# A two-part transformer kernel on one core: four edits around a joint feed-forward stage

## The chip, the cores and the metric

The kernel runs on 1 core of a Trainium2 chip, as one program and one launch. The metric is device time in microseconds (us), the median over runs. PE is the matrix engine, DVE the vector engine, ACT the scalar engine, POOL and SP here only issue DMAs.

## The reference, cut to what matters

There are 256 tokens of 1024 features (`x`) and 256 context tokens (`ctx`), all in fp32. Two models run one after the other; only the first has a context.

```
s_lat, s_ctx = silu(c), silu(c_ctx)
for l in 0, 1:                                  # first model
    six vectors for x from s_lat @ w_ada[l], six for ctx from s_ctx @ w_ada[l]
    h  = rmsnorm(x) * gain * (1 + scale) + shift             # the same for ctx
    conv branch: glu, depthwise conv, layernorm, silu;  attention branch over x and ctx
    x  = x + g1 * ((sigmoid gates * branches) @ w_out)       # ctx too where l = 0
    x  = x + g2 * (silu(u_g) * u_a) @ w_down,  u = conv3(norm(x) @ w_up)   # ctx too where l = 0
x = rmsnorm(x)
for l in 0, 1:                                  # second model
    half a swiglu, stick-breaking attention (l = 0) or a gated recurrence (l = 1), half a swiglu,
    each modulated by vectors from silu(c_2) @ mod_w[l]
return rmsnorm(x)
```

The vectors are small in output and large in weights: `s @ w_ada` and `s @ mod_w` read 120 blocks of 1 MB, which the kernel calls modulation blocks.

## The kernel before

**Matrix work.** Activations lie features by tokens. A weight is read in slabs, each of two halves. For each half ACT rounds the raw fp32 weights to a high part (`split_hi`, L744), DVE subtracts it from the raw ones for a low part (`split_lo`, L1333), and PE makes three matmuls for each 128x128 chunk: high by high, high by low, low by high (`mm3`, L2206 to L2208). Raw weights, high parts and low parts have two buffers each (slab parity p). SP loads the next raw half once the low part of the one before in its buffer is made. Each engine runs through one list of stages (`plan`) in the same order, with its own code for every stage kind. There is no scheduler: the order in which the code is written is the order on the engine, and a wait holds all that stands behind it.

**Modulation blocks.** Blocks 0 to 21 are multiplied on PE. From block 22 on each half block is one DVE instruction (`mod_product`, L1370: a 128x1024 multiply with a sum) on `modraw`, which has one buffer for each half; blocks below 32 need a second one for the context (L1367). POOL loads the next block's half into the buffer once the product of this half is done. A stage's `mods` says how many blocks it takes: 1 is one half block with each slab, 2 both halves. A product that finds its half not landed holds DVE.

**The places.** (a) The gated stage of the context (kind `gate`): attention heads beside the gate slabs, then a layernorm of the conv branch, whose four Silu on ACT (L1053) free the last chunks of the first `merge` slab. (b) A norm needs the sum of squares over 8 feature tiles. ACT squares, DVE adds some of the tiles (`add_squares`, L1524), and PE sums over partitions with a matrix of ones (`norm_sum`, L2261, fp32, one matmul for each tile that is left). Two norms of `x` are made ahead, during other stages: one in the context's `merge` stage, one in the stages `q` and `v` that make keys and values of the context for layer 1 (`norm_ahead`). (c) The joint feed-forward of layer 0 runs `x` and `ctx` together (512 columns) in two parts: 12 features of 22 through `upa` and `down`, then the other 10. In `upa` each slab gives one feature: ACT scales (L1172, L1174), DVE adds four conv taps (L2032), ACT takes a Silu (L1159), DVE multiplies (L2004), ACT rounds (L1180, for the last L1190), DVE makes the low part (L2010). The last two steps of a feature follow the taps of the next one. `joint_opening` is the first two slabs of `down` on PE. (d) In the last body of the second `down` part (`ctx_first`), PE makes the context's halves of slabs 6 and 7 first, then `x` of 6, the norm's sum, and `x` of 7. The norm of the context follows (`do_norm`, i = 4): root, eight scaled tiles (L1504), high parts on ACT (L833), low parts on DVE (L1513), for the keys' slab (`slab_after_norm`, L2533 to L2542). DVE's update of the residual is `joint_product` (L1888). (e) Stage `q` with `w_sbk` and stage `v` with `w_sbv` make keys and values of the stick-breaking attention. In the latter DVE's masks and sums (L1694, L1684, L1699) stand between the low parts and the modulation products.

## Time and profile before

| | us |
|---|---|
| median of 3 runs (2250.38 to 2251.74) | 2250.89 |
| the profiled execution | 2255.51 |
| its span, first to last instruction | 2253.5 |
| PE busy in it | 2167.5 (96%) |
| DVE busy | 1808.6 (80%) |
| ACT busy | 1246.7 (55%) |

The share of PE's clock that is granted is 0.986 over the span: it stands at 1.0 (2.4 GHz) or at 0.5 (1.2 GHz). Matmul ends are modelled, so a busy PE says less than the starts of its instructions and its idle times. An idle time is printed in brackets behind the instruction that ends it, with what released it.

### The profile page before, as it was taken

Reading aid. Unit: us, or ns where it says so; the run is one execution under the profiler, and the core shown is the slowest. Engines: PE = TensorE matmul, PEld = TensorE weight load, DVE = VectorE, ACT = ScalarE, POOL = GpSimd, SP = SyncE. Lnnn points to the kernel's source line nnn. Section 1 sums busy time; section 2 is a strip of 40 time slices with the busy share of each in tenths; the row PEclk is TensorE's granted clock in tenths of the full one; section 3 lists DMA queues with packets and bytes.
Section 4 is the critical chain, followed back from the end, with each engine's and each line's share of the span. In section 5 each row is a group of like instructions: output and inputs, shape, how many; then the busy total and the mean of one; then the engine's idle time right before and its main releaser. Section 6 shows DMA issues by size and latency. Waiting matters only on the chain.

```text
span 2253.5 us, 42557 instructions
## 1 busy us (share of the span) xinstructions
PE 2167.5 (96%) x15168; PEld 1984.7 (88%) x15168; DVE 1808.6 (80%) x3102; ACT 1246.7 (55%) x1981; POOL 120.4 (5%) x232
## 2 busy tenths in 40 slices
PE   7998999999999989999999999999999999999998
PEld 5897988888788779889999889997989989999898
DVE  4886797777677768978998988877988888889865
ACT  4466457544223333576664664656664655686653
POOL 0100000000010100000000001000010001000000
PEclk8999999999999999999999999999999999999999
DMA  9845553434475555535788688773788788636754
GB/s 360 284 132 172 182 175 127 151 130 133 137 261 184 180 178 172 178 118 166 239 271 275 227 282 266 231 245 122 246 277 272 230 280 279 232 125 192 243 177 132
DMA packets 139741, 465.59 MB, mean 207 GB/s; under 512 B 16208, under 2 KB 20432, under 8 KB 138064
## 3 DMA queue, kind: packets, MB, share of 16 engines
q1 hardware_dynamic: 102560, 339.41, 44.8%
q0 software_dynamic: 32688, 120.08, 17.1%
q10 hardware_dynamic: 4352, 4.20, 0.6%
q8 instruction: 92, 1.51, 0.3%
q14 instruction: 49, 0.40, 0.0%
HBM read 462.57 MB, written 1.05 MB: 206 GB/s over the span
## 4 chain that ended last, share of the span: by engine, by line
PE 74%; DVE 12%; ACT 6%; issue 4%; DMA 3%; ACTq 0%; SPq 0%; DVEq 0%; POOL 0%; POOLq 0%
PE bank_pair L2206 16%; PE bank_pair L2208 16%; PE bank_pair L2207 16%; PE bank_pair L2345 12%; PE bank_pair L2350 6%; DVE w_lo L1333 3%; DMA modraw<-in_w_mod 2%; DVE arena L1648 2%; ACT w_hi L744 2%; PE bank_pair L2335 2%; DVE small L1762 1%; PE ps_o L2219 1%; ACT arena L1011 1%; DVE arena L1823 1%; PE ps_o L2853 1%
## 5 line engine op out<-in xcount | busy, mean ns | idle before, releaser
L1333 DVE TENSOR_TENSOR w_lo<-raw,w_hi 128x1024 fp32r<-128x1024 f32 (+2 forms) x672 | 735.5, 1118 | 124.8 <-ACT w_hi L744 120.3
L744 ACT ACTIVATE w_hi<-raw 128x1024 fp32r<-128x1024 f32 (+2 forms) x672 | 640.5, 969 | 334.2 <-PE bank_pair L2208 193.1
L2206 PE MATMUL bank_pair<-e_both,w_hi 128*128 128x256 f32 (+1 forms) x1632 | 470.9, 289 | 11.3 <-DVE w_lo L1333 7.7
L2206 PE MATMUL bank_pair<-h_joint,w_hi 128*128 128x256 f32 (+1 forms) x1488 | 464.5, 312 | 8.1 <-DVE w_lo L1333 3.4
L2207 PE MATMUL bank_pair<-e_both,w_hi 128*128 128x256 f32 (+1 forms) x1632 | 464.1, 284 | 0.0
L2208 PE MATMUL bank_pair<-e_both,w_lo 128*128 128x256 f32 (+1 forms) x1632 | 464.0, 284 | 0.0
L2207 PE MATMUL bank_pair<-h_joint,w_hi 128*128 128x256 f32 (+1 forms) x1488 | 456.7, 307 | 0.0
L2208 PE MATMUL bank_pair<-h_joint,w_lo 128*128 128x256 f32 (+1 forms) x1488 | 456.5, 307 | 0.0
L2206 PEld LDWEIGHTS bank_pair<-e_both,w_hi 128*128 128x128 f32 x1632 | 314.9, 193 | 22.0 <-DVE w_lo L1333 9.9
L2207 PEld LDWEIGHTS bank_pair<-e_both,w_hi 128*128 128x128 f32 x1632 | 315.2, 193 | 0.3
L2208 PEld LDWEIGHTS bank_pair<-e_both,w_lo 128*128 128x128 f32 x1632 | 315.0, 193 | 0.0
L2206 PEld LDWEIGHTS bank_pair<-h_joint,w_hi 128*128 128x128 f32 x1488 | 285.4, 192 | 33.2 <-issue 14.1
L2345 PE MATMUL bank_pair<-h_joint,w_hi 128*128 128x512 f32 x1216 | 304.6, 393 | 0.1
L2207 PEld LDWEIGHTS bank_pair<-h_joint,w_hi 128*128 128x128 f32 x1488 | 285.7, 192 | 12.9
L2208 PEld LDWEIGHTS bank_pair<-h_joint,w_lo 128*128 128x128 f32 x1488 | 285.5, 192 | 12.4
L1370 DVE SCALAR_TENSOR_TENSOR modraw<-modraw,cact 128x1024 f32<-128x1024 f32 x196 | 238.1, 1220 | 32.5 <-DMA modraw<-in_w_mod 32.2
L2345 PEld LDWEIGHTS bank_pair<-h_joint,w_hi 128*128 128x128 f32 x1216 | 218.8, 189 | 39.2 <-DVE e_plain L1473 0.3
L693 POOL DMA_DIRECT2D modraw<-in_w_mod x216 | 114.1, 529 | 1954.2 <-DVE modraw L1370 1742.0
L2350 PEld LDWEIGHTS bank_pair<-h_joint,w_lo 128*128 128x128 f32 x1216 | 165.9, 191 | 11.8
L2350 PE MATMUL bank_pair<-h_joint,w_lo 128*128 128x256 f32 x1216 | 169.6, 283 | 0.0
L1648 DVE SCALAR_TENSOR_TENSOR arena<-arena,par 128x256 f32<-128x256 f32 x360 | 149.8, 479 | 4.0 <-PE bank_pair L2807 3.8
L2032 DVE SCALAR_TENSOR_TENSOR arena<-bank_pair,par,arena 128x510 f32<-128x510 f32 (+1 forms) x168 | 93.0, 621 | 47.8 <-ACT arena L1174 47.6
(258 smaller groups left out, 2636.1 us busy)
## 6 DMA issues: line engine op xcount, KB each, us to landing
modraw<-in_w_mod POOLq DMA_DIRECT2D x216, 512.0 KB, 5.2
raw<-in_w_gu SPq DMA_DIRECT2D x176, 512.0 KB, 5.5
raw<-in_w_up SPq DMA_DIRECT2D x88, 512.0 KB, 5.4
raw<-in_w_gate SPq DMA_DIRECT2D x48, 512.0 KB, 4.1
raw<-in_w_dn SPq DMA_DIRECT2D x64, 384.0 KB, 4.8
raw<-in_w_dn SPq DMA_DIRECT2D x64, 320.0 KB, 4.0
raw<-in_w_glu SPq DMA_DIRECT2D x24, 512.0 KB, 5.4
raw<-in_w_merge SPq DMA_DIRECT2D x24, 512.0 KB, 3.7
```

Source lines behind the costliest of these rows:

```text
L693: nc.gpsimd.dma_start(modraw[:, c, :], a["w_mod"][m, :, D * c:D * (c + 1)]).then_inc(mod_in[c], 16)
L744: nc.scalar.activation(w_hi[:, p, HALF * f:HALF * f + w], raw[:, p, HALF * f:HALF * f + w], ACT.Copy)\
L1333: nc.vector.tensor_tensor(w_lo[:, p, at], raw[:, p, HALF * f:HALF * f + w], w_hi[:, p, at].bitcast(F32), ALU.subtract).then_inc(lo_ready, 1)
L1370: nc.vector.scalar_tensor_tensor(out=modraw[:, p, :], in0=modraw[:, p, :], scalar=1.0, in1=cact[:, int(second_block), :], op0=ALU.mult, op ...
L1648: ins = nc.vector.scalar_tensor_tensor(out=o, in0=u, scalar=w[:, j, t:t + 1], in1=o, op0=ALU.mult, op1=ALU.add)
L2032: nc.vector.scalar_tensor_tensor(out=o, in0=i_, scalar=taps[:, c, 0:1] if left else taps[:, c, 2:3], in1=o, op0=ALU.mult, op1=ALU.add)\
L2206: nc.tensor.matmul(out, l[0], r[0], start=start, stop=False)
L2207: nc.tensor.matmul(out, l[0], r[1], start=False, stop=False)
L2208: return nc.tensor.matmul(out, l[1], r[0], start=False, stop=stop)
L2335: ins = nc.tensor.matmul(pb[p][:, f, 0:T], raw[:, p, c:c + P], h_plain[:, k, :], start=k == 0, stop=k == DC - 1)
L2345: nc.tensor.matmul(pb[p][:, f, :].rearrange("p (e t) -> p e t", e=2), w_hi[:, p, c:c + P], h_sides[:, :, k, :], start=k == 0, stop=False)
L2350: ins = nc.tensor.matmul(pb[p][:, f, T:2 * T], w_lo[:, p, c:c + P], h_hi[:, k, :], start=False, stop=k == DC - 1)
```

## The change

Six things are done. **(1)** In `joint_opening` PE no longer waits for the last feature but one before it starts: the chunks of the last two features of slab 0 come after the first half of slab 1. **(2)** In a joint `upa` stage the modulation products of the last slab move behind the last feature's multiply and low part. **(3)** The Silu of the vectors (`cact`, 128x2048) moves in the context's gated stage from behind the first gates' sigmoid to ahead of the layernorm's Silus. **(4)** For the two norms of `x` that are made ahead, DVE adds no squares: PE sums all 8 tiles (8 matmuls of ones for 1). **(5)** The second `down` part takes 3 blocks for 6, one half block with each of its first six slabs; one of the other blocks goes to the layer 1 stage `v` of the context, two to the `w_sbk` stage, which now takes two half blocks with each slab as the `w_sbv` stage does. **(6)** The last `joint_product` of `x` in the second `down` part moves from ahead of the context norm's root to behind its scaled tiles.

```diff
             stage("down", ..., n * P, 4, kc=n,
-                  mods=2, mods_last=3 if part else 4, joint=True, part0=part0,
+                  mods=2 - part, mods_last=3 if part else 4, joint=True, part0=part0,
...
-    stage("v", a["w_v1"], SLAB, 1, arg=dict(dst="vc", conv=None, heads=NA_H))
+    stage("v", a["w_v1"], SLAB, 1, mods=1, arg=dict(dst="vc", conv=None, heads=NA_H))
...
-    stage("q", a["w_sbk"], SLAB, 2, mods=1, arg=dict(dst="sbk", ...))
+    stage("q", a["w_sbk"], SLAB, 2, mods=2, arg=dict(dst="sbk", ...))
...
             if s.mods == 1:
-                s.mods_to = s.mods_to or s.bodies
+                s.mods_to = s.mods_to or s.mods_last or s.bodies
...
                 s["adds"] = {"out": DC - 3, "down": DC - 2}[s["fused"]] if s["fused"] else DC - 1
+                if s["x"] == "x" and s["kind"] == "a" and s["v"] == 0:
+                    s["adds"] = 0
...
+            def vectors_silu():
+                act.wait_ge(vec_in[1], 16)
+                nc.scalar.activation(cact[:], cact[:], ACT.Silu).then_inc(c_ready, 1)
...
+                if i == 0:
+                    vectors_silu()
                 for k in range(CONV_C):
                     act.wait_ge(ln_scaled, CONV_C * i + k + 1)
                     link(nc.scalar.activation(ln_y[:, k, :], cy[:, k, :], ACT.Silu, ...))
...
                 open_gates(0)
-                if i == 0:
-                    act.wait_ge(vec_in[1], 16)
-                    nc.scalar.activation(cact[:], cact[:], ACT.Silu).then_inc(c_ready, 1)
...
-                    if slot in (1, 2):
+                    if slot in (1, 2) and n["adds"]:
                         for k in range(4 * slot - 3, min(4 * slot + 1, DC)):
                             add_squares(n, k)
...
-                if n["fused"] and n["before"].joint:
-                    joint_product(n["before"], DC - 1, 1, "x")
-                elif n["fused"]:
+                if n["fused"] and not n["before"].joint:
...
                 dve.wait_ge(std_ready, i + 1)
-                wait_up(dve, updated, n["x0"])
+                if n["fused"] and n["before"].joint:
+                    dve.wait_ge(updated, updated_at(n["before"], DC - 1, "ctx"))
+                else:
+                    wait_up(dve, updated, n["x0"])
...
                 scaled(n, range(DC))
                 if i == 4:
+                    joint_product(n["before"], DC - 1, 1, "x")
                     split_lo(second(n["before"]), 0)
...
                     step(b, 1, last, True, folded)
-                    mods(s, b, 1, is_first, last)
+                    if not (s.joint and last):
+                        mods(s, b, 1, is_first, last)
                 sweep(dve, s, body)
                 n = 2 * s.bodies
                 tail_mul(s.e0 + n, 1)
                 tail_lo(s.e0 + n, 1, n - 1)
+                if s.joint:
+                    mods(s, s.bodies - 1, 1, False, True)
...
                 if p == 0:
-                    pe.wait_ge(up_lo, up_done[id(s)] + FC - 1)
+                    pe.wait_ge(up_lo, up_done[id(s)] + FC - 2)
...
-                    for k in range(n, 2 * n - 1):
+                    for k in range(n, 2 * n - 2):
                         chunk(0, k)
                     free_banks(s, 0, 1, True)
                     pe.wait_ge(lo_ready, 2 * s.l0 + 3)
                     for k in range(n):
                         chunk(1, k)
                     pe.wait_ge(up_lo, up_done[id(s)] + FC)
+                    chunk(0, 2 * n - 2)
                     chunk(0, 2 * n - 1).then_inc(half_done, 1)
...
             def norm_sum(n):
-                pe.wait_ge(sq_added, n["adds0"] + n["adds"])
+                wait_up(pe, sq_added, n["adds0"] + n["adds"])
```

ACT at the end of the context's gated stage, before: `cact` are the vectors, `e_plain` the gates and the layernorm's values, `modrow` a modulation row.

```order
L1055 ACTIVATE e_both<-e_plain 128x256
L1064 ACT_TABLE_LOAD
L1064 ACTIVATE e_plain<-e_plain 128x2x512
L1059 ACT_TABLE_LOAD
L1059 ACTIVATE cact<-cact 128x2048
L744 ACTIVATE w_hi<-raw 128x1024 x2
L760 ACTIVATE modrow<-ps_o 128x256
L1077 ACTIVATE e_both<-arena 128x256
L1064 ACT_TABLE_LOAD
L1064 ACTIVATE e_plain<-e_plain 128x2x512
L1077 ACTIVATE e_both<-arena 128x256
L855 ACTIVATE arena<-x_res 128x256 x8
```

The same place now (the changed file's line numbers are higher by 2 to 10):

```order
L1047 ACT_TABLE_LOAD
L1044 ACTIVATE e_both<-ps_o 128x128
L755 ACTIVATE cact<-cact 128x2048
L1063 ACTIVATE e_plain<-arena,par 128x256
L1065 ACTIVATE e_both<-e_plain 128x256
...
L1071 ACT_TABLE_LOAD
L1071 ACTIVATE e_plain<-e_plain 128x2x512
L746 ACTIVATE w_hi<-raw 128x1024 x2
L768 ACTIVATE modrow<-ps_o 128x256
L1084 ACTIVATE e_both<-arena 128x256
L1071 ACTIVATE e_plain<-e_plain 128x2x512
L863 ACTIVATE arena<-x_res 128x256 x8
```

The vectors' Silu stands ahead of the layernorm's, in a table that is there already, and two table loads are gone.

DVE from the last feature of the second `upa` part into the second `down` part, before:

```order
L2032 SCALAR_TENSOR_TENSOR arena<-bank_pair,par,arena 128x2x255 x4
L2010 TENSOR_TENSOR e_joint<-arena,e_joint 128x512
L1370 SCALAR_TENSOR_TENSOR modraw,modcol<-modraw,cact 128x1024 x2
L2004 TENSOR_TENSOR arena<-arena 128x512
L2010 TENSOR_TENSOR e_joint<-arena,e_joint 128x512
L1333 TENSOR_TENSOR w_lo<-raw,w_hi 128x640 x2
L1370 SCALAR_TENSOR_TENSOR modraw,modcol<-modraw,cact 128x1024 x2
L1888 SCALAR_TENSOR_TENSOR ctx_res<-bank_pair,cols,ctx_res 128x256
L1888 SCALAR_TENSOR_TENSOR x_res<-bank_pair,cols,x_res 128x256
```

And now:

```order
L2041 SCALAR_TENSOR_TENSOR arena<-bank_pair,par,arena 128x2x255 x4
L2019 TENSOR_TENSOR e_joint<-arena,e_joint 128x512
L2013 TENSOR_TENSOR arena<-arena 128x512
L2019 TENSOR_TENSOR e_joint<-arena,e_joint 128x512
L1377 SCALAR_TENSOR_TENSOR modraw,modcol<-modraw,cact 128x1024 x2
L1340 TENSOR_TENSOR w_lo<-raw,w_hi 128x640 x2
L1377 SCALAR_TENSOR_TENSOR modraw,modcol<-modraw,cact 128x1024
L1897 SCALAR_TENSOR_TENSOR ctx_res<-bank_pair,cols,ctx_res 128x256
L1897 SCALAR_TENSOR_TENSOR x_res<-bank_pair,cols,x_res 128x256
```

The two products pass the last feature's two steps, and from here on a `down` slab of this part has one product for two; the products still stand ahead of the slab's update.

DVE from the second `down` part's end through the context's norm to the norm of `x`, before:

```order
L1888 SCALAR_TENSOR_TENSOR x_res<-bank_pair,cols,x_res 128x256
L1495 SCALAR_TENSOR_TENSOR arena<-ps_t,arena 128x256
L1497 SCALAR_TENSOR_TENSOR arena<-arena 128x256
L1499 SCALAR_TENSOR_TENSOR arena<-arena 128x256
L1504 SCALAR_TENSOR_TENSOR arena<-ctx_res,cols,arena 128x256 x8
L1333 TENSOR_TENSOR w_lo<-raw,w_hi 128x1024
L1513 SCALAR_TENSOR_TENSOR h_joint<-arena,cols,h_joint 128x256 x8
L1333 TENSOR_TENSOR w_lo<-raw,w_hi 128x1024 x2
L1524 TENSOR_TENSOR arena<-arena 128x256 x7
L1333 TENSOR_TENSOR w_lo<-raw,w_hi 128x1024 x2
```

And now:

```order
L1502 SCALAR_TENSOR_TENSOR arena<-ps_t,arena 128x256
L1504 SCALAR_TENSOR_TENSOR arena<-arena 128x256
L1506 SCALAR_TENSOR_TENSOR arena<-arena 128x256
L1511 SCALAR_TENSOR_TENSOR arena<-ctx_res,cols,arena 128x256 x8
L1897 SCALAR_TENSOR_TENSOR x_res<-bank_pair,cols,x_res 128x256
L1340 TENSOR_TENSOR w_lo<-raw,w_hi 128x1024
L1520 SCALAR_TENSOR_TENSOR h_joint<-arena,cols,h_joint 128x256 x8
L1340 TENSOR_TENSOR w_lo<-raw,w_hi 128x1024 x4
```

The root (three instructions) no longer stands behind the last update of `x`, and the seven additions of squares are gone.

## Rows read from the trace of the kernel before

**Rows 1.** Page: busy times; group of products; issue of their loads, us to landing.

```profile
PE 2167.5 (96%) x15168; PEld 1984.7 (88%) x15168; DVE 1808.6 (80%) x3102; ACT 1246.7 (55%) x1981; POOL 120.4 (5%) x232
...
L1370 DVE SCALAR_TENSOR_TENSOR modraw<-modraw,cact 128x1024 f32<-128x1024 f32 x196 | 238.1, 1220 | 32.5 <-DMA modraw<-in_w_mod 32.2
...
modraw<-in_w_mod POOLq DMA_DIRECT2D x216, 512.0 KB, 5.2
```

**Rows 2.** Timeline, PE: start us, us, instruction [idle before it, releaser]; seven waits.

```profile
191.19 0.41 PE L2228 MATMUL ps_t<-tab,modrow 128*128 128x128 f32 x2 [4.33 <-DVE modcol L1340]
...
204.78 0.48 PE L2261 MATMUL ps_t<-arena,tab 128*128 128x256 f32 x1 [3.33 <-DVE arena L1524]
...
583.49 0.77 PE L2206 MATMUL bank_pair<-e_joint,w_hi 128*128 128x512 f32 x1 [4.93 <-DVE arena L2032]
...
764.64 0.47 PE L2206 MATMUL bank_pair<-e_joint,w_hi 128*128 128x512 f32 x1 [4.93 <-DVE arena L2032]
...
814.24 0.58 PE L2206 MATMUL bank_pair<-e_joint,w_hi 128*128 128x256 f32 x1 [3.32 <-DVE x_res L1888]
...
831.68 0.36 PE L2533 MATMUL bank_pair<-h_joint,w_hi 128*128 128x256 f32 x1 [3.18 <-ACT h_joint L833]
...
844.49 0.80 PE L2261 MATMUL ps_t<-arena,tab 128*128 128x256 f32 x1 [3.00 <-DVE arena L1524]
```

**Rows 3.** Windows: stretch, its us, busy by engine, granted clock, DMA share, GB/s.

```profile
191.59:195.01 3.42, 3.42 (x24) 2.17 (x24) 2.65 (x6) 3.41 (x7) 1.05 (x2) 0.50 0.74 246
205.25:208.66 3.41, 3.41 (x18) 3.33 (x17) 3.19 (x6) 1.37 (x2) 0.00 (x0) 0.50 0.92 330
580.71:587.54 6.83, 4.05 (x10) 3.21 (x11) 6.14 (x11) 1.85 (x3) 0.53 (x1) 0.50 0.03 12
765.03:768.45 3.42, 3.42 (x10) 2.64 (x9) 2.73 (x6) 0.98 (x2) 1.05 (x2) 0.50 0.21 56
812.82:819.65 6.83, 5.41 (x25) 5.41 (x26) 2.92 (x7) 2.74 (x4) 0.53 (x1) 0.50 0.54 172
843.54:850.37 6.83, 5.88 (x25) 5.70 (x26) 4.75 (x10) 3.12 (x5) 0.00 (x0) 0.50 0.60 196
```

**Rows 4.** Timeline, ACT, end of the context's gated stage and first merge slab.

```profile
184.49 1.28 ACT L1059 ACT_TABLE_LOAD   x1
185.79 1.91 ACT L1059 ACTIVATE cact<-cact 128x2048 f32<-128x2048 f32 x1
...
194.00 2.55 ACT L855 ACTIVATE arena<-x_res 128x256 f32<-128x256 f32 x8
```

**Rows 5.** Chain in order of time, another norm's sum: three tiles, six records.

```profile
247.19 1.29 PE ps_t L2261 x6
```

**Rows 6.** Timeline, PE, end of the first joint up part.

```profile
577.94 0.39 PE L2207 MATMUL bank_pair<-h_joint,w_hi 128*128 128x512 f32 x1
578.16 0.39 PE L2208 MATMUL bank_pair<-h_joint,w_lo 128*128 128x512 f32 x1
```

**Rows 7.** Timeline, DVE, both joint openings and the second down part's end.

```profile
586.98 0.69 DVE L2010 TENSOR_TENSOR e_joint<-arena,e_joint 128x512 fp32r<-128x512 f32 x1 [0.69 <-ACT e_joint L1190]
...
764.46 1.22 DVE L1370 SCALAR_TENSOR_TENSOR modraw<-modraw,cact 128x1024 f32<-128x1024 f32 x1
...
812.16 1.23 DVE L1370 SCALAR_TENSOR_TENSOR modraw<-modraw,cact 128x1024 f32<-128x1024 f32 x1 [3.49 <-DMA modraw<-in_w_mod]
...
825.24 1.23 DVE L1333 TENSOR_TENSOR w_lo<-raw,w_hi 128x1024 fp32r<-128x1024 f32 x1 [0.18 <-ACT w_hi L744]
828.53 0.48 DVE L1888 SCALAR_TENSOR_TENSOR x_res<-bank_pair,cols,x_res 128x256 f32<-128x256 f32 x1 [2.07 <-PE bank_pair L2208]
```

**Rows 8.** Windows: the stage of `w_sbk`, columns as in Rows 3.

```profile
1470.00:1496.00 26.00, 26.00 (x218) 25.70 (x217) 17.95 (x30) 12.76 (x14) 2.11 (x4) 1.00 0.81 266
```

**Rows 9.** Timeline, DVE, second halves of two blocks in the `w_sbv` stage.

```profile
1499.48 1.23 DVE L1370 SCALAR_TENSOR_TENSOR modraw<-modraw,cact 128x1024 f32<-128x1024 f32 x1 [1.54 <-DMA modraw<-in_w_mod]
...
1509.37 1.23 DVE L1370 SCALAR_TENSOR_TENSOR modraw<-modraw,cact 128x1024 f32<-128x1024 f32 x1 [2.40 <-DMA modraw<-in_w_mod]
```

More of the change, by code:

```diff
@@ L189, in ffn_joint @@
             stage("upa", a["w_up0"], SLAB, n // 2, mods=1 + part, arg=dict(l=0), joint=True, j0=j0)
[L190 removed]
+            stage("down", a[f"w_down0{part}"], n * P, 4, kc=n, mods=2 - part, mods_last=3 if part else 4, joint=True, part0=part0,
                   arg=dict(x="ctx", kind="a", l=0, v=5, need=N_MOD_A, part=part))
```

3 lines of the change are left out of this document (1 added, 2 removed).

## The prediction

> **What bounds the kernel now.** I read the page first. PE is busy 96% of the span, DVE 80%, ACT 55% [rows 1], so work taken from DVE or ACT is worth something only where PE stands and waits for it. The next view is therefore the timeline of PE, and in it the idle times in brackets. Seven of them lie where the change works [rows 2]: 4.33 in the context's gated and `merge` stages, 3.33 ahead of the norm sum there, 4.93 at each of the two openings of the joint `down` parts, 3.32 in the second `down` part, 3.18 in the context's norm, 3.00 ahead of the sum in the stage `v` of layer 1. Together they are 27.0 us. In all but one the releaser is DVE.
>
> The third view is the table of windows, and it shows that an idle time costs more than itself. Around or behind six of the seven a window stands at a granted clock of 0.50, that is 1.2 GHz [rows 3]. Work done there at half speed takes twice its time, so half of PE's busy time in a window is loss: 1.7 of 3.42 behind the wait at 191.19, 1.7 of 3.41 behind that at 204.78, 2.0 of 4.05, 1.7 of 3.42, 2.7 of 5.41 and 2.9 of 5.88 in the other four. That is 12.7 in all. A wait removed should give back its window too, if PE is then kept fed.
>
> **The change part by part.** Gains are positive.
>
> *A, gated stage and `merge` (edits 3 and 4).* Behind the sigmoid ACT loads a table (1.28) and takes the vectors' Silu (1.91) ahead of the high parts at 187.60 [rows 4]. Now the load is gone, and the Silu stands ahead of the layernorm's four, so that its 1.91 pushes these and the sigmoid. The high parts come 1.28 earlier if all of it is passed on, 3.19 if none. The lower end is the nearer one: ACT shows no idle time in these rows that could take 1.91 up. A second table load further on goes too. PE's wait of 4.33 thus shrinks and does not vanish, and the next turn of the stage still holds for ACT's eight squares of 2.55 [rows 4]; I count 1.5 for wait and first window together (0 to 4.9, which is 3.19 and the 1.7 of the window). At the sum, PE's wait of 3.33 and one tile of 0.48 [rows 2] give way to eight tiles. Another norm's three tiles take 1.29 [rows 5], so eight take 3.44. ACT's squares end at 196.55, long before. That gives 0.4, and the window behind it 1.7. **A = 3.6** (0.4 to 7.0).
>
> *B, first opening (edits 1 and 2).* The `up` part ends on PE at 578.56, which is 583.49 less 4.93 [rows 2]. A chunk is three matmuls that start 0.22 apart [rows 6], 0.68 with rounding. PE can now do ten chunks of slab 0 and six of slab 1, 10.9 us, before it needs the last feature, which means 589.5. That low part ends at 587.67 today [rows 7] and, with two products of about 1.2 [rows 1] behind it and not ahead, at about 585.4. The cover holds with 4 us to spare. Gain: 4.93 and the window's 2.0. **B = 6.9** (4.9 to 6.9).
>
> *C, second opening.* The same edits give 4.93 and 1.7. But here a product follows with the first slab, and the block's two halves are freed later. The last feature's multiply takes the place of the product at 764.46 [rows 7]; multiply, ACT's rounding and low part take 0.69 each by the nearest row, 586.98 and its bracket [rows 7], to 766.5. Product to 767.7, about 0.6 until POOL issues, landing 5.2 later [rows 1], product to 774.7, two updates of 0.48 [rows 7], pipelined, to 775.6. PE begins at 759.7 and fills two slabs of 10 chunks in 13.6 us, so it wants the bank at 773.3. The new wait of 2.3 stands on DVE's product with the slab's updates queued behind it. **C = 4.3** (2.0 if the wait is twice as long; 6.6 without it).
>
> *D, second `down` part (edit 5).* The wait of 3.32 at 814.24 is DVE's update of `x`, and DVE's own row shows why: its product at 812.16 waited 3.49 for its half to land [rows 7], with the update behind. With one half for each slab, a half has two slabs to come in (13.6 us by the chunks above) and needs 5.2 and a product of 1.2. The wait goes, with its window's 2.7. **D = 6.0** (3.3 to 6.0).
>
> *E, context norm (edit 6).* DVE begins the root only when the last product of `x` is added, at 828.53 for 0.48, after a wait of 2.07 for PE; its low part before that ended at 826.47 [rows 7]. The root can start 2.5 earlier. The update of 0.48 now stands between the scaled tiles and the low parts, on the way to PE's wait of 3.18 [rows 2]. **E = 2.1** (0, if the sum's root on ACT or the high parts end last, to 2.5).
>
> *F, sum ahead in stage `v` of layer 1.* The wait of 3.00 and a tile of 0.80 [rows 2] give way to eight tiles, 3.44: 0.4, and the window's 2.9. Two products of 1.2 each [rows 1] come to DVE where seven additions leave it, so I cost them at nothing; if PE runs out of low parts behind one of them, it costs its 1.2. **F = 3.3** (−0.8 to 3.3).
>
> *G, the `w_sbk` stage (edit 5).* This is what the rest is paid with. The stage takes four more half blocks, 4 x 512 KB = 2.1 MB [rows 1], in a stretch where PE never rests and the DMA engines are already 0.81 busy at 266 GB/s [rows 8]: 6.9 MB in 26.0 us become 9.0. If the engines filled up (266/0.81 = 328 GB/s) the stretch would last 27.5; at the same 266 it would last 33.9. The lag is 1.5 or 7.9. Elsewhere 330 GB/s at a share of 0.92 stands in the row of 205.25 [rows 3], which speaks against the higher figure; the transfers of the halves that wait for a product before they start speak against the lower. I take the middle, 4.7, as 5. The ends: nothing, if buffered slabs cover it; and the pace of the stage behind, where two halves are taken with each slab: its second halves follow each other by 9.9 us and each waits for its DMA, 1.54 and 2.40 [rows 9]. Four slabs at 9.9 for 6.5 make 13.6. A late half holds DVE, behind it the low parts, behind them PE. **G = −5** (−13.6 to 0).
>
> At two places a page says something of its own. The Trainium skill, "ScalarE: Activation LUTs", section "What ACT_TABLE_LOAD costs", has a switch of tables at about 1283 ns of load and 1380 ns of drain. The load agrees with the row's 1.28, but the Silu starts at 185.79, right behind 184.49 and 1.28, so the trace shows no drain there; by the page A would be up to 2.8 larger and the time about 2227.
>
> **The sum.** 3.6 + 6.9 + 4.3 + 6.0 + 2.1 + 3.3 = 26.2, less 5 is 21.2. The profiled execution took 2255.5 with a span of 2253.5; by it the changed span would be 2232.3 and its execution 2234.3. The profiled one lies 4.6 over the median of the runs, so the time I forecast is 2250.9 − 21.2 = **2230**.
>
> **Rivals.**
> *1. `w_sbk` costs nothing.* DVE is busy 17.95 of 26.0 there [rows 8], low parts are made ahead in two buffers, and the halves' first transfers are long in. Against it: the rate above. 2225. The Trainium skill, "DMA: Bandwidth & Descriptors", section "Specifications", gives about 358 GB/s of HBM for a core; 9.0 MB would pass in 25.2 us, and the stretch would not grow. The row's 330 at a share of 0.92 agrees with that figure; none in `w_sbk` shows it.
>
> *2. The clock stays at half.* The waits become shorter (A, C, E keep some), and six windows in the trace stand around waits of 3 to 5 us; whether waits of 1 or 2 spare the clock these rows do not say. If every window that I count as gone but the first stays, 1.7 + 2.0 + 1.7 + 2.7 + 2.9 = 11.0 are lost: 2241.
>
> *3. The openings end on another wait.* PE would then stand at slab 1's second half or at the bank, with the low parts of weights late, since DVE's products now stand ahead of that half's `w_lo`. B and C give nothing: 11.2 lost, 2241. Against it: 4 us of cover in B.
>
> *4. Slower than before: the halves' turnaround in `w_sbk`.* If a half needs a time t from product to product with each slab, four slabs cost 4(t − 6.5). That eats the gain of 26.2 from t = 13.1 on. The longest in rows is 9.9 [rows 9], with a lower load. At t = 14 the time is 2255.
>
> *5. The second and part of the fourth together:* the clock stays at half, 11.0, and `w_sbk` lags by 11, 6 more than counted; 4 us are left: 2247.
>
> **How the numbers follow.** Forecast 0.46, rivals 1 to 5: 0.17, 0.18, 0.08, 0.05, 0.06. The forecast's own spread, its terms taken as independent, is some 6 down and 9 up. The range takes in rivals 1 to 3: 2219 (2225 less 6) to 2242. Within 0.2%, 4.5 us, is about what a measurement can tell from no change. Faster is forecast and rivals 1 to 3, 0.89; rival 5 is the same, 0.06; rival 4 is slower, 0.05.
>
> **What the changed profile would show.** A and F: no DVE releaser at the two norm sums, eight tiles each, PE's wait near 191 under 3. B: no wait at 583, last features behind slab 1's first half. C: a new wait of about 2 on PE near 773, a DVE product that waits for its DMA. D: no such product wait at 812. E: the root ahead of the last `x` update, PE's 3.18 near 1. The windows of rows 3 at 1.00. G: DVE waiting for `modraw` in `w_sbk`, PE waiting behind late low parts, a longer stage with a higher rate. If G's stage grows by over 14 us, or the clock stays at 0.50 behind the sums, I am wrong.

## The result, and the profile after

| | median, us | range | ratio to the kernel before, 95% interval |
|---|---|---|---|
| the kernel before, 5 runs | 2250.89 | 2248.81 to 2252.79 | |
| the changed kernel, 5 runs | 2239.00 | 2236.88 to 2240.07 | 0.9944 (0.9933 to 0.9956) |
| the kernel before, in the next set, 9 runs | 2250.42 | 2248.31 to 2255.69 | |
| the changed kernel again, 4 runs | 2236.3 | 2234.55 to 2237.01 | 0.9932 (0.9916 to 0.9947) |

The change is faster by 11.9 us, and by 14.1 in a second set of runs, which is 0.5 to 0.6%. The forecast was 21.2, to 2230, in a range of 2219 to 2242. The page of the changed kernel has these lines for those of [rows 1] (busy times; the group of products; the issues of their loads with the median time to landing):

```profile
PE 2167.1 (97%) x15196; PEld 1983.0 (89%) x15196; DVE 1802.9 (81%) x3088; ACT 1244.7 (56%) x1979; POOL 120.4 (5%) x232
...
L1377 DVE SCALAR_TENSOR_TENSOR modraw<-modraw,cact 128x1024 f32<-128x1024 f32 x196 | 237.9, 1219 | 34.8 <-DMA modraw<-in_w_mod 34.4
...
modraw<-in_w_mod POOLq DMA_DIRECT2D x216, 512.0 KB, 5.3
```

PE's busy time is the same to 0.4 us while the span fell from 2253.5 to 2238.0. DVE's waits for landed halves did not fall: 32.2 became 34.4. They moved. The timeline of PE shows where its own went; these are the waits that it has left at the seven places of [rows 2], the new ones, and the one at 1231, which was 1.64 in the first profile of the kernel before:

```profile
182.00 0.39 PE L2218 MATMUL bank_pair<-e_both,w_hi 128*128 128x256 f32 x1 [0.67 <-DVE e_both L1814]
...
190.18 0.41 PE L2240 MATMUL ps_t<-tab,modrow 128*128 128x128 f32 x2 [1.50 <-DVE modcol L1347]
...
198.97 0.41 PE L2240 MATMUL ps_t<-tab,modrow 128*128 128x128 f32 x2 [1.44 <-DVE modcol L1347]
...
764.92 0.50 PE L2218 MATMUL bank_pair<-e_joint,w_hi 128*128 128x512 f32 x1 [0.95 <-DVE x_res L1897]
...
808.08 0.36 PE L2546 MATMUL bank_pair<-h_joint,w_hi 128*128 128x256 f32 x1 [0.43 <-ACT h_joint L841]
...
1231.36 0.80 PE L2273 MATMUL ps_t<-arena,tab 128*128 128x256 f32 x1 [2.69 <-ACT arena L1100]
...
1480.59 0.49 PE L2687 MATMUL ps_t<-arena 64*128 64x256 f32 x2 [2.60 <-DVE arena L1703]
...
1489.28 0.49 PE L2687 MATMUL ps_t<-arena 64*128 64x256 f32 x2 [1.83 <-DVE arena L1703]
```

Five of the seven waits are gone altogether (both sums, the first opening, the second opening's first wait, the second `down` part). The context norm keeps 0.43 of 3.18, the gated stage 1.50 of 4.33. The 0.67 at 182.00, which ends on a low part of the layernorm's Silu, is new, and so are the 1.44 at 198.97, the 0.95 at the bank of slab 2 and those at 1480 and 1489, behind DVE's masks. The windows at the places of [rows 3], in the same order, and two more, at 1231 and 1489 (columns as there, the clock third from the end):

```profile
191.00:195.50 4.50, 4.50 (x45) 4.09 (x38) 1.95 (x5) 3.25 (x11) 1.05 (x2) 1.00 0.80 279
199.00:203.00 4.00, 4.00 (x30) 2.84 (x31) 2.96 (x6) 2.75 (x5) 1.06 (x2) 1.00 0.70 226
575.00:588.00 13.00, 13.00 (x59) 10.76 (x58) 9.15 (x16) 4.74 (x8) 0.53 (x1) 1.00 0.31 112
760.00:772.00 12.00, 11.05 (x48) 8.62 (x47) 9.79 (x20) 3.58 (x6) 1.59 (x3) 1.00 0.87 272
806.00:820.00 14.00, 13.56 (x95) 12.29 (x95) 11.15 (x22) 9.88 (x21) 0.00 (x0) 1.00 0.47 147
836.00:850.00 14.00, 13.69 (x115) 13.58 (x114) 13.23 (x23) 9.15 (x15) 1.06 (x2) 1.00 0.75 236
1231.30:1235.00 3.70, 3.64 (x11) 3.10 (x12) 2.35 (x4) 1.75 (x4) 0.00 (x0) 0.50 0.43 143
1489.71:1493.12 3.41, 3.41 (x14) 2.20 (x11) 1.06 (x2) 2.07 (x3) 0.53 (x1) 0.50 0.79 262
```

All six places now stand at 1.00, that is 2.4 GHz. The last two lines are stretches at 0.50 that the first profile of the kernel before did not have there; the one at 1489 lies behind a wait that the change itself brings.

**Where the time went, place by place.** The start of the same PE instruction is read in two traces; by how much their difference changes from one end of a place to the other is what the change did there. For example, the instruction that started at 560.03 started at 557.11 in the changed kernel, 2.92 earlier, and the one at 592.04 started at 582.04, 10.00 earlier: the first opening gave 7.1. I did this twice, with the first profiles of both kernels and with a second profile of each (gains positive, us):

| place, in the first trace of before | forecast | first pair | second pair |
|---|---|---|---|
| A, gated stage and `merge`, 170 to 209 | 3.6 | 3.3 | 1.9 |
| B, first opening, 560 to 592 | 6.9 | 7.1 | 8.0 |
| C, second opening, 750 to 786 | 4.3 | 5.3 | 6.0 |
| D, rest of the second `down` part, 805 to 823 | 6.0 | 5.9 | 0.4 |
| E, context norm, 823 to 841 | 2.1 | 2.3 | 2.9 |
| F, sum in stage `v`, 841 to 854 | 3.3 | 2.9 | 1.7 |
| end of the first half swiglu, 1225 to 1270 | none | −3.6 | 1.9 |
| G, `w_sbk` and `w_sbv`, 1450 to 1516 | −5 | −7.1 | −6.7 |
| all else | none | −0.7 | −3.1 |
| from the first to the last instruction, about | 21.2 | 15.4 | 13.0 |

The second pair's total lies between the differences of the medians, 11.9 and 14.1; the first pair's is larger. The forecast had been worked out from the one execution of the kernel before that the first pair uses, and it is close to that pair place by place.

### The profile page after: what moved, and what is told of

It reads as the page before. It is cut to its first block, busy times and chain, and to the rows that moved or that the text cites. A ratio compares the mean times of both kernels' runs of the same rounds, so it can differ in the third digit from the quotient of the medians.

```text
span 2238.0 us, 42579 instructions
## 1 busy us (share of the span) xinstructions
PE 2167.1 (97%) x15196; PEld 1983.0 (89%) x15196; DVE 1802.9 (81%) x3088; ACT 1244.7 (56%) x1979; POOL 120.4 (5%) x232
## 4 chain that ended last, share of the span: by engine, by line
PE 73%; DVE 12%; ACT 6%; DMA 4%; issue 4%; ACTq 0%; DVEq 0%; SPq 0%; POOL 0%; POOLq 0%
PE bank_pair L2218 16%; PE bank_pair L2220 15%; PE bank_pair L2219 15%; PE bank_pair L2357 12%; PE bank_pair L2362 6%; DVE w_lo L1340 3%; DMA modraw<-in_w_mod 2%; DVE arena L1657 2%; ACT w_hi L746 2%; PE bank_pair L2347 2%; PE ps_t L2273 1%; DVE small L1771 1%; PE ps_o L2231 1%; ACT arena L1019 1%; PE ps_o L2866 1%
## 5 line engine op out<-in xcount | busy, mean ns | idle before, releaser
L2218 PEld LDWEIGHTS bank_pair<-h_joint,w_hi 128*128 128x128 f32 x1488 | 284.2, 191 | 33.3 <-issue 14.1
L1377 DVE SCALAR_TENSOR_TENSOR modraw<-modraw,cact 128x1024 f32<-128x1024 f32 x196 | 237.9, 1219 | 34.8 <-DMA modraw<-in_w_mod 34.4
L2362 PEld LDWEIGHTS bank_pair<-h_joint,w_lo 128*128 128x128 f32 x1216 | 165.9, 190 | 11.9
```

Source lines behind the costliest of these rows:

```text
L1377: nc.vector.scalar_tensor_tensor(out=modraw[:, p, :], in0=modraw[:, p, :], scalar=1.0, in1=cact[:, int(second_block), :], op0=ALU.mult, op ...
L2218: nc.tensor.matmul(out, l[0], r[0], start=start, stop=False)
L2362: ins = nc.tensor.matmul(pb[p][:, f, T:2 * T], w_lo[:, p, c:c + P], h_hi[:, k, :], start=False, stop=k == DC - 1)
```

## The experiments

All times are medians of the timed runs. "Against the changed kernel" means against 2236.3 and 2239.0, its two medians.

**The two kernels again.** Neither is altered.

> The kernel before once more, nothing altered: 2250 within 2. Its first profiled execution, 2255.5, lay 4.6 over the median, and the sum of the prediction was made against it. Theory: that execution lost 3 to 4 us at places the change does not touch, so that this profile, if it lies nearer the median, differs from the first in single stretches at 0.50 or at single waits, and the seven waits that the change works on (27.0 together) and their windows are the same. Rival: the seven waits themselves vary by some us, and the first profile had them long.

> The changed kernel once more, nothing altered: 2239 within 2. In its first profile PE waited 2.69 at 1231.36, ahead of the norm sum at the end of the first half swiglu of the second model, and a stretch at a granted clock of 0.50 stood behind it; the kernel before waited 1.64 at the same place and kept its clock, which left it 3.3 us better there. Theory one, that this is chance of one execution (the two waits differ by transfers that landed up to a microsecond later): the place looks different in this profile, wait 1.6 to 2.7, with or without the stretch. Theory two, that the change moves it for good: the same 2.7 and 0.50 again. The wait of about 1 us at 765 and those of 1.5 at 190 and 199 come back under both.

The kernel before took 2251.5 (10 runs), the changed one 2236.3, just under the 2237 to 2241 that I expected. The second profile of the kernel before has a span of 2245.5, 8.0 under its first, and not only at places that the change leaves alone, as I had expected: the rival was right in part. These are the waits of its PE at the first norm sum, at the context norm and at the second sum, and the one at 1248:

```profile
203.97 0.48 PE L2261 MATMUL ps_t<-arena,tab 128*128 128x256 f32 x1 [2.12 <-DVE arena L1524]
...
824.26 0.36 PE L2533 MATMUL bank_pair<-h_joint,w_hi 128*128 128x256 f32 x1 [3.19 <-ACT h_joint L833]
...
837.59 0.48 PE L2261 MATMUL ps_t<-arena,tab 128*128 128x256 f32 x1 [2.99 <-DVE arena L1524]
...
1248.06 0.70 PE L2261 MATMUL ps_t<-arena,tab 128*128 128x256 f32 x1 [2.30 <-ACT arena L1093]
```

Five of the seven waits are those of [rows 2] to 0.01: 4.33, 4.93, 4.93, 3.19 and the second sum's 2.99. The first sum's has 2.12 where it had 3.33. DVE's squares are ready as early as before, but PE comes 1.2 later, because behind the 4.33 its clock stands at 0.50 until 196.8 where it had been back at 1.00 at 195.0. And the wait of 3.32 at 814.24, on which D rested, is down to 0.17. The issue of the load of that half block, first profile and second (KB, us from issue to landing), DVE's row of the product that waits for it (it answers to 812.16 in [rows 7]), and the window in which the slow clock had stood show the reason:

```profile
modraw<-in_w_mod POOLq DMA_DIRECT2D x1, 512.0 KB, 6.9
...
modraw<-in_w_mod POOLq DMA_DIRECT2D x1, 512.0 KB, 4.0
```

```profile
807.10 1.23 DVE L1370 SCALAR_TENSOR_TENSOR modraw<-modraw,cact 128x1024 f32<-128x1024 f32 x1 [1.04 <-DMA modraw<-in_w_mod]
```

```profile
811.00:819.00 8.00, 8.00 (x66) 7.89 (x66) 4.01 (x6) 3.84 (x7) 0.00 (x0) 1.00 0.42 143
```

The same load of the same kernel took 6.9 in one execution and 4.0 in the other, and the product waited 3.49 and 1.04 for it. In the first PE stood for it and lost its clock; in the second neither.

The place at 1231 is chance too. In the second profile of the changed kernel the same wait is 1.47 and no slow stretch follows; in the second profile of the kernel before, 2.30 with one. Theory one stands. The wait ends on ACT's squares (L1093, L1100), but further back along ACT a transfer stands: the high parts of `w_gu` ahead of these squares wait for raw weights, 0.31 for the last of them in the first profile of the kernel before, 1.37 in the first of the changed one:

```profile
1248.61 1.06 ACT L744 ACTIVATE w_hi<-raw 128x1024 fp32r<-128x1024 f32 x1 [0.31 <-DMA raw<-in_w_gu]
```

```profile
1224.67 1.06 ACT L746 ACTIVATE w_hi<-raw 128x1024 fp32r<-128x1024 f32 x1 [1.37 <-DMA raw<-in_w_gu]
```

A landing behind the wait is seen in all 14 traces; that it sets the wait's length is not tested. The loss of 7 in `w_sbk` comes back, in other waits (3.70 and 1.03) and again with a stretch at 0.50, this time behind the first:

```profile
1227.78 0.48 PE L2273 MATMUL ps_t<-arena,tab 128*128 128x256 f32 x1 [1.47 <-ACT arena L1100]
...
1476.40 0.49 PE L2687 MATMUL ps_t<-arena 64*128 64x256 f32 x2 [3.70 <-DVE arena L1703]
...
1494.57 0.49 PE L2687 MATMUL ps_t<-arena 64*128 64x256 f32 x2 [1.03 <-DVE arena L1703]
```

```profile
1477.50:1480.91 3.41, 3.41 (x18) 3.41 (x18) 1.66 (x5) 1.44 (x2) 0.53 (x1) 0.50 0.87 257
```

**What `w_sbk` pays for.** First the loads alone were cut to an eighth; this kernel leaves out the other seven eighths of these blocks, and its result is not the right one:

```
-            with pool.Fori(N_BOTH + 4, N_MOD) as m:
+            with pool.Fori(N_BOTH + 4, 81) as m:
...
+            for m in range(81, 89):
+                for c in range(2):
+                    pool.wait_ge(mod_done, 2 * m - 1 + c)
+                    nc.gpsimd.dma_start(modraw[:, c, 0:P], a["w_mod"][m, :, D * c:D * c + P]).then_inc(mod_in[c], 16)
...
```

> The changed kernel with the loads of blocks 81 to 88 (those issued during w_sbk and w_sbv) cut to an eighth, 128 of 1024 columns; every product is still made over the full half, so these blocks' vectors are not the right ones. It parts the transfers from DVE's work. Theory: the lag of 7.0 in w_sbk and w_sbv is the halves' transfers; 2232, no wait of DVE for modraw there, PE's waits of 2.60 and 1.83 at 1480 and 1489 gone. Rival: it is the four more products of 1.2 us each on DVE, 4.9 us, that make the masks late: 2237 to 2239 with the PE waits still there.

2228.0 (2227.6 to 2231.5, 4 runs), 4 under the theory's 2232, which had been reckoned from 2239.0; it is 8.3 under 2236.3. By the starts of PE's instructions, 1450 to 1516 of the kernel before now costs 0.0 (21.36 earlier at both ends) with the same twelve products on DVE. So the lag is the transfers, not DVE's work. The second halves' products in the changed kernel, on DVE's timeline, show how it arises:

```profile
1452.38 1.22 DVE L1377 SCALAR_TENSOR_TENSOR modraw<-modraw,cact 128x1024 f32<-128x1024 f32 x1
...
1461.72 1.23 DVE L1377 SCALAR_TENSOR_TENSOR modraw<-modraw,cact 128x1024 f32<-128x1024 f32 x1 [1.59 <-DMA modraw<-in_w_mod]
...
1469.54 1.23 DVE L1377 SCALAR_TENSOR_TENSOR modraw<-modraw,cact 128x1024 f32<-128x1024 f32 x1 [2.77 <-DMA modraw<-in_w_mod]
...
1476.16 1.23 DVE L1377 SCALAR_TENSOR_TENSOR modraw<-modraw,cact 128x1024 f32<-128x1024 f32 x1 [1.55 <-DMA modraw<-in_w_mod]
...
1494.58 1.23 DVE L1377 SCALAR_TENSOR_TENSOR modraw<-modraw,cact 128x1024 f32<-128x1024 f32 x1 [3.82 <-DMA modraw<-in_w_mod]
```

There are six of them (one at 1483.98 is left out), all but the first behind a wait. From 1452.38 to 1494.58 they take 42.2, 8.4 for each round of product, reload and landing, where a slab of `w_sbk` had taken 6.5 [rows 8]. PE does not stand in `w_sbk` itself, whose low parts were made ahead. It stands one stage later, at 1480 and 1489, where DVE's masks come behind the late products. These two waits sum to 4.4; the rest of the 7.1 is mostly the stretch at 0.50 behind the second, which costs 1.7 as half of its 3.41 busy. In the second pair it is 3.70, 1.03 and again 1.7. The window of the stage shows that the DMA engines did not fill up:

```profile
1448.00:1474.00 26.00, 25.75 (x216) 25.38 (x215) 17.65 (x31) 12.81 (x14) 3.17 (x6) 1.00 0.75 248
```

0.75 busy at 248 GB/s is less than the 0.81 and 266 of [rows 8], before four halves were added. My reading is that a half that can only be asked for once its product is done leaves the engines idle in between.

**Where else the two blocks could go.** They were put into two stages of layer 1 of `x`, with `w_sbk` back at one half for each slab:

```
-        stage("merge", a[f"w_merge{l}"], SLAB, 2, mods=2 * early)
+        stage("merge", a[f"w_merge{l}"], SLAB, 2, mods=2 if early else int(l == 1))
```

> The changed kernel with the two blocks that went to the w_sbk stage put into the merge stage of layer 1 of x (a half block with each of its four slabs), so that w_sbk has one half with each slab again. Theory: the 7.0 us that PE loses between 1494 and 1517 (against the kernel before, by the same instructions) come from the halves' loads in w_sbk, and the merge stage, where DMA is 0.40 busy and DVE 35 of 50 us, takes them for nothing: 2232, 7 less than the changed kernel, and no DVE wait for modraw over 2.5 in w_sbk. Rival one: the lag belongs to the w_sbv stage whatever comes ahead: 2239. Rival two: the merge stage loses as much: 2239, with new waits of PE near 1000.

```
-        stage("out", a[f"w_out{l}"], SLAB, 2, mods=int(early), turn_end=early,
+        stage("out", a[f"w_out{l}"], SLAB, 2, mods=int(early or l == 1), turn_end=early,
```

> The changed kernel with the two blocks of w_sbk in the out stage of layer 1 of x (a half block with each slab). In the merge stage, which I tried, the products stood between the gated sums that PE waited for, and 5.5 of the 6.7 us were lost again there. In the out stage DVE has only low parts and updates. Theory: the loss in w_sbk and w_sbv goes and nothing takes its place: 2230 to 2232. Rival: a product there delays the update or the low part as in merge, three or four waits of about 1.1: 2234 to 2236.

In `merge` 2234.9 (2234.0 to 2235.8, 5 runs), in `out` 2233.3 (2231.2 to 2235.4, 5 runs; 0.9927 of the kernel before, 0.9912 to 0.9942). In both the loss of 7 at `w_sbk` is gone (0.0 from 1450 to 1516), and in both most of it is lost again where the blocks went, 5.5 and 4.9, by new waits and a stretch at 0.50 at the last of them (1013.27 to 1016.68 and 1035.84 to 1039.25). Both times lie between the theory and the rival: in `merge` rival two has the mechanism, in `out` the loss has the rival's size though not its kind. PE in `merge` (the first of three equal waits, and the last), then in `out`:

```profile
993.92 0.39 PE L2218 MATMUL bank_pair<-e_both,w_hi 128*128 128x256 f32 x1 [1.14 <-DVE arena L1832]
...
1013.42 0.58 PE L2218 MATMUL bank_pair<-e_both,w_hi 128*128 128x256 f32 x1 [2.30 <-DVE w_lo L1340]
```

```profile
1035.10 0.48 PE L2273 MATMUL ps_t<-arena,tab 128*128 128x256 f32 x1 [2.07 <-ACT arena L1100]
```

In `merge` a product stands between DVE's gated sums. In `out` there is one new wait, at the norm sum behind the stage. 2233.3 is the lowest median of a kernel that computes the whole result, but its interval overlaps that of the changed kernel, so I don't call it faster.

**All blocks back (edit 5 undone).**

```
-                  mods=2 - part, mods_last=3 if part else 4, joint=True, part0=part0,
+                  mods=2, mods_last=3 if part else 4, joint=True, part0=part0,
...
-    stage("v", a["w_v1"], SLAB, 1, mods=1, arg=dict(dst="vc", conv=None, heads=NA_H))
+    stage("v", a["w_v1"], SLAB, 1, arg=dict(dst="vc", conv=None, heads=NA_H))
...
-    stage("q", a["w_sbk"], SLAB, 2, mods=2, arg=dict(dst="sbk", rope=False, scale=1.0, conv=None))
+    stage("q", a["w_sbk"], SLAB, 2, mods=1, arg=dict(dst="sbk", rope=False, scale=1.0, conv=None))
```

> The changed kernel with its move of blocks undone: six blocks in the second down part again, none in stage v, two in w_sbk. Theory: w_sbk gives back 7.0, the second down part loses its 5.9 (a product that waits for its half near 800, PE 3 us behind it with a stretch at 0.50); together 2238. At the second opening, where the bank of slab 2 waits for a product, two products instead of one stand ahead of the update, so PE waits over 2 and not 1: up to 2 more, 2240. Rival: the gain in the second down part came with the earlier openings and not from the blocks: 2232.

2237.8 (4 runs), as the theory had it, but its parts were not those I expected. 1450 to 1516 costs 0.0. The second `down` part's end keeps 5.0 of the 5.9 against the first trace of before; the wait there is 0.64. So the rival is right about this place, if not about the time: the gain there does not need the fewer blocks. What is lost is the second opening, 750 to 786, which gives −0.5 instead of 5.3. The timelines of PE and DVE there:

```profile
768.40 0.80 PE L2218 MATMUL bank_pair<-e_joint,w_hi 128*128 128x512 f32 x1 [4.88 <-DVE x_res L1897]
```

```profile
762.35 1.22 DVE L1377 SCALAR_TENSOR_TENSOR modraw<-modraw,cact 128x1024 f32<-128x1024 f32 x1 [1.91 <-DMA modraw<-in_w_mod]
766.33 1.22 DVE L1377 SCALAR_TENSOR_TENSOR modraw<-modraw,cact 128x1024 f32<-128x1024 f32 x1 [2.75 <-DMA modraw<-in_w_mod]
```

With six blocks two products, both waiting for halves, stand ahead of slab 0's update; PE waits 4.88 for it. So, with the products behind the last feature, the fewer blocks are what lets the second opening keep its gain. Edit 5 as a whole buys about 5.8 there and 0.9 behind it, and pays 7.1: nothing, within what these runs tell.

**The openings.** Edit 1 is these lines, and edit 2 the place of the products in `upa`; each experiment reverses or adds them:

```
-                    pe.wait_ge(up_lo, up_done[id(s)] + FC - 2)
+                    pe.wait_ge(up_lo, up_done[id(s)] + FC - 1)
...
-                    for k in range(n, 2 * n - 2):
+                    for k in range(n, 2 * n - 1):
...
-                    chunk(0, 2 * n - 2)
                     chunk(0, 2 * n - 1).then_inc(half_done, 1)
...
-                    if not (s.joint and last):
-                        mods(s, b, 1, is_first, last)
+                    mods(s, b, 1, is_first, last)
...
-                if s.joint:
-                    mods(s, s.bodies - 1, 1, False, True)
```

> The changed kernel with edits 1 and 2 undone: PE waits for the last feature but one at both joint openings, and the two products of the last up slab stand ahead of that feature again. The changed kernel took 2236.3 to 2239.0. Theory: both openings give 7.1 and 5.3 by the traces, so 2249 to 2251, with waits of 4.9 at 583 and 760 and stretches at a granted clock of 0.50 behind them. Rival: the cover at the second opening only moved a wait to slab 2's bank (0.9 us in the changed kernel), which the old order would not have; then the second gives under 4 and it is 2246.

> The changed kernel with edit 2 alone undone: PE takes the last two features late, but the two modulation products stand ahead of the last feature on DVE again. By the prediction's cover the last feature is then needed at 589.5 at the first opening and made at 587.7, so nothing is lost there; at the second it is needed 8.8 us after PE's start, 768.5 in the time of the kernel before, and made at 768.8, so a wait of 0.3 to 1 stands there, while the halves are freed 2.3 earlier and the wait of 0.9 at the bank of slab 2 goes. Theory: same as the changed kernel within 1, 2236 to 2239. Rival: the last low part of weights, behind the products, ends later than it did and PE waits 2 or more at both openings: 2241 or more.

> The kernel before with edit 1 alone: PE takes the last two features late, the products stay ahead of the last feature, six blocks stay in the second down part. It tests what the bank of slab 2 waits for. With six blocks and the products behind the last feature, PE waited 4.9 at that bank; here the halves come free 2.3 earlier. Theory, the reload of the halves sets that wait: 2.6 there, so the second opening gives 4.9 and 1.7 less 2.6 and some 0.3, 3.7; the first gives 7.1; 2250.4 less 10.8 is 2239 to 2241. Rival, that wait is set by DVE's products and not by the reload: 4.9 again, 2242 to 2243; or by the block of the three in the changed kernel alone: under 1, 2237.

With both undone: 2250.5 (10 runs), 11.5 to 14.2 over the changed kernel and the same as the kernel before (1.0004, 0.9995 to 1.0014). What is left of the change in that kernel is edits 3 to 6, so by the clock these together give nothing that the runs tell, and the openings are the whole gain. The waits are those of [rows 2] again:

```profile
578.79 0.77 PE L2215 MATMUL bank_pair<-e_joint,w_hi 128*128 128x512 f32 x1 [4.93 <-DVE arena L2041]
...
760.33 0.76 PE L2215 MATMUL bank_pair<-e_joint,w_hi 128*128 128x512 f32 x1 [4.94 <-DVE arena L2041]
```

With edit 2 alone undone: 2235.1 (2234.6 to 2237.4, 4 runs), the same as the changed kernel, so edit 1 carries the openings and edit 2 adds nothing. No wait stands at the first opening, one of 0.34 at the second, as the cover said, and the wait at slab 2's bank is gone:

```profile
758.90 0.50 PE L2215 MATMUL bank_pair<-e_joint,w_hi 128*128 128x512 f32 x1 [0.34 <-DVE e_joint L2019]
```

With edit 1 alone on the kernel before: 2244.0 (2239.9 to 2246.8, 7 runs), 3 over the theory's upper end. The bank of slab 2, for which I expected 2.6, waits 0.39, and the late feature 0.33, but three further waits follow:

```profile
768.01 0.50 PE L2206 MATMUL bank_pair<-e_joint,w_hi 128*128 128x512 f32 x1 [0.39 <-DVE x_res L1888]
...
777.02 0.50 PE L2206 MATMUL bank_pair<-e_joint,w_hi 128*128 128x512 f32 x1 [1.91 <-DVE x_res L1888]
...
792.59 0.50 PE L2206 MATMUL bank_pair<-e_joint,w_hi 128*128 128x512 f32 x1 [1.61 <-DVE x_res L1888]
...
805.43 0.39 PE L2206 MATMUL bank_pair<-e_joint,w_hi 128*128 128x256 f32 x1 [2.14 <-DVE x_res L1888]
```

They sum to 6.1, near the 4.88 and 0.64 with the products behind. Ahead of each stands a product that waits for its half, for 0.27 to 3.51. My estimate of one reload was too local, and neither rival had the waits that came. In both traces with six blocks and an early start of PE, PE stands for the reloads somewhere, nearly at once or in four pieces; with the three blocks of edit 5 only 0.95 is left.

**The other three edits, each undone.** Edit 4 (DVE adds squares again), edit 3 (the Silu behind the first gates), edit 6 (the update ahead of the root):

```
-                if s["x"] == "x" and s["kind"] == "a" and s["v"] == 0:
-                    s["adds"] = 0
```

> The changed kernel with edit 4 undone: DVE adds seven tiles of squares for the two norms of x made ahead, PE sums one. Theory: waits of 3.0 to 3.3 come back at the two sums near 201 and 837, each with a stretch at 0.50 behind it; by windows 1.7 and 2.9, by the exchange of a wait and a tile for eight tiles 0.4 each: 5 in all, 2241 to 2244. Rival: without the three products of old in the second down part DVE is ahead at the second sum, and only the first comes back: 2238.5 to 2241.

```
-                if i == 0:
-                    vectors_silu()
                 for k in range(CONV_C):
...
                 open_gates(0)
+                if i == 0:
+                    vectors_silu()
```

> The changed kernel with edit 3 undone: the vectors' Silu behind the first gates again, with its two table loads. Theory: PE's wait at 190 grows from 1.5 to 4.3 with a stretch at 0.50 behind it (1.7), part of which the later turn at 199 gives back (its wait of 1.4 shrinks): 1.5 to 3 lost, 2238 to 2242. Rival, that edit 3 gives the whole of wait and window: 4.5 lost, 2241 to 2243.5. Rival, that it gives nothing, since the next turn waits for ACT's squares all the same: 2236 to 2239 and the wait at 199 gone.

```
-                if n["fused"] and not n["before"].joint:
+                if n["fused"] and n["before"].joint:
+                    joint_product(n["before"], DC - 1, 1, "x")
+                elif n["fused"]:
...
                 if i == 4:
-                    joint_product(n["before"], DC - 1, 1, "x")
                     split_lo(second(n["before"]), 0)
```

> The changed kernel with edit 6 undone: the last product of x is added ahead of the context norm's root again. The changed kernel took 2236.3 and 2239.0. Theory: PE's wait ahead of the context's high parts grows from 0.43 to 3.2 (it was 3.18), 2.5 lost: 2239 to 2241.5. Rival: with the second down part faster the root was held by something else, and under 1 is lost: 2236 to 2239.5.

PE with the sums back (two rows), with the Silu back, and with the update back:

```profile
202.80 0.79 PE L2271 MATMUL ps_t<-arena,tab 128*128 128x256 f32 x1 [3.33 <-DVE arena L1529]
...
822.30 0.79 PE L2271 MATMUL ps_t<-arena,tab 128*128 128x256 f32 x1 [2.99 <-DVE arena L1529]
```

```profile
190.76 0.66 PE L2240 MATMUL ps_t<-tab,modrow 128*128 128x128 f32 x2 [4.33 <-DVE modcol L1347]
```

```profile
808.94 0.36 PE L2544 MATMUL bank_pair<-h_joint,w_hi 128*128 128x256 f32 x1 [3.19 <-ACT h_joint L841]
```

Every wait returns at its old length. By the starts of PE's instructions against the second profile of the changed kernel, the sums cost 2.4 and 1.6, the Silu 1.5, the update 2.4. By the clock of the runs they cost less surely: 2239.9, 2239.0 and 2242.6, which is 0.9 to 3.6, 0 to 2.7 and 3.6 to 6.3 over the changed kernel. The last is 1.1 over its theory; its one trace also has the stretch at 1231, which is worth 3.7 there. With the sums back the time lies under the theory's 2241, in the rival's numbers, but the rival's mechanism is refuted, since both waits are back. With the Silu back the wait at 199 is gone, as the second rival said, but not the whole gain: the 1.5 is the lower end of the theory.

The trace also shows what edit 3 does. With the Silu back PE runs 1.4 earlier through the matmuls ahead of the wait (the 0.67 at 182.00 is gone), then waits 4.33 for 1.50, loses 1.4 to a clock at 0.50, and has 1.4 back where the wait at 199 was. So edit 3 does not shorten the waiting: 4.33 becomes 1.4, 1.50 and 1.44 in three pieces, because the Silu now holds the layernorm ahead. Its gain is the clock, which stays at 1.00.

## Why the prediction was right, and where it was not

**Right: which waits end, and what each carries.** B, C, E and F came out within 1.7 of the forecast in both pairs, and undoing edits 1 and 2 alone brings the whole time back. C's new wait was 0.95 for the 2.3 of the sum. The slow clock behind the first opening returned what half the busy time of its window said (7.1 less 4.93 is 2.1, forecast 2.0); with the sums back the first costs 2.4 (2.1 in the sum) and the second 1.6 (3.3 in the sum). In A the 1.5 for edit 3 was met to the tenth, but as the clock alone: the sum had the wait shorter, and it was only spread. The larger A that stands beside the sum, for a drain at each table load, did not come.

**Inside its range, and short.** 2239.0 and 2236.3 lie inside 2219 to 2242, nearer to the 2241 of rivals 2 and 3, whose mechanisms did not happen, than to 2230. The forecast had 11.2 for the openings and 10.0 for all else (3.6 + 6.0 + 2.1 + 3.3 − 5). With the openings undone, by the clock, nothing of that 10.0 is left. In that kernel's trace against the second profile of before A, D, E and F give 1.9, 0.4, 2.9 and 1.7, G takes 5.8, and the spans are 2245.7 and 2245.5.

**Wrong: D, the step "the wait goes, with its window's 2.7", 6.0.** The wait was a product held by a DMA, and I took its length in one execution for a property of the kernel. The second execution of the same code has 1.04 on DVE, 0.17 on PE and no slow window, and D gives 0.4. The bounds of 3.3 to 6.0 did not hold that. That the first pair has 5.9 is luck of the execution. The tell was in the rows: of seven waits this was the only one whose cause, one step back on DVE, was a landing and not an instruction. The six others end on engines, and five of them came back within 0.01 in the second profile.

**Wrong: the base.** The sum was made against an execution 4.6 over the median and then subtracted from the median. Of the 8.0 us that the second one was shorter, 5.5 lie between 805 and 823 (1.9 ahead at the one end, 7.4 at the other), at the very wait that D priced. Against the second execution D would have been priced near nothing; how many of the timed runs had the wait is not known, since they have no trace. D's 6.0 for 0.4 is most of the distance from 21.2 to the 13.0 of the second pair; the rest is G and pieces of one to three microseconds that I cannot place.

**Right in kind, with a term left out: G.** 5 was taken between 1.5 and 7.9, and 6.7 and 7.1 were measured. In both pairs 1.7 of that is the stretch at 0.50 behind PE's new waits. The sum gave back such a stretch with the waits that it took away and counted none for the waits that G brings. Without it the lag is 5.0 and 5.4, and that this is the 5 of the sum is luck: it was the middle of two rates, and neither set the pace. The halves' rounds of 8.4 did, and the rate fell to 248. So the limit that the Trainium skill gives ("DMA: Bandwidth & Descriptors", "Specifications", about 358 GB/s of HBM for a core), by which nothing would be lost, was not what bound this stage, and rival 1 fell. Rival 4 had the mechanism; its price of 4(t − 6.5) is 7.6 with t = 8.4, too much for the lag alone.

**Not priced: the stretch at 1231.** The place was outside the change, and 3.6 was lost there in the first pair and 1.9 gained in the second. A forecast has to carry some 3 us of such chance on either side in this kernel.

**The rivals.** Rival 2, the clock stays at half, did not happen at any of the six places; behind 1.50 and 1.44 the clock stood at 1.00. Rival 3, another wait at the openings, happened in small (0.95), and with six blocks it happens in full at the second (4.88).

**Left open.** Why medians of the changed kernel differ by 2.7 between two sets of runs is not settled; the stretch at 1231, in one of its two profiles and not in the other, is of that size, but the timed runs have no trace.

## What to carry to other kernels

Follow a wait back along the engines before pricing it. Here five of seven came back within 0.01 in a second execution. One a step behind a DMA (3.32 and 0.17) did not, nor did one that ends on ACT with a landing further back (1.64 and 2.30 in the kernel before), nor one behind a slow stretch that lasted longer (3.33 and 2.12). Such a wait has to be seen in a second execution before it is priced, and the base of the sum should be an execution like the median one. When loads can be asked for only after their buffer is used, price them by the round of use, reload and landing at that place, not by free bandwidth; look for the loss one stage later, and add the stretch at half clock that the new wait may bring. And one long wait cut into three short ones can pay by the clock alone.

## What was not expected of the hardware

The length of a wait does not by itself say whether the clock falls behind it. At the norm sum near 1231 two kernels waited 2.31, with blocks and with the Silu undone; PE's timeline and the window behind it in each:

```profile
1237.18 0.70 PE L2273 MATMUL ps_t<-arena,tab 128*128 128x256 f32 x2 [2.31 <-ACT arena L1100]
```

```profile
1237.20:1241.00 3.80, 3.80 (x27) 3.65 (x28) 2.46 (x4) 1.67 (x3) 0.00 (x0) 1.00 0.46 147
```

```profile
1231.94 0.79 PE L2273 MATMUL ps_t<-arena,tab 128*128 128x256 f32 x1 [2.31 <-ACT arena L1100]
```

```profile
1231.94:1235.00 3.06, 3.06 (x8) 2.52 (x9) 1.80 (x3) 1.70 (x3) 0.00 (x0) 0.50 0.48 174
```

The first pair is the kernel with the old blocks: 1.00, 27 matmuls in 3.8 us. The second is the one with the Silu back: 0.50, 8 matmuls in 3.1. In the 14 traces six waits of 1.03 to 1.71 kept the clock at this place, and of the eight from 2.21 to 2.69 all lost it but the 2.31 of the first pair. At `w_sbv` the changed kernel's first profile has the two in reverse: the 2.60 at 1480.59 kept the clock at 1.00 until the next wait, and behind the 1.83 at 1489.28 it fell.
